# One 512-column matmul for the high and low activations in the dense units of a hybrid encoder block's RWKV pairs

## The reference

```
xn   = rms_norm(h, norm_pre_mix)
cols = xn @ w_in                     # q | k | v | r k v + LoRA-down (RWKV-7) | two merge gates
o_attn = banded_gqa_attention(q, k, v, sink)
o_rwkv = rwkv7_bidirectional(rw_cols, ...)   # token shift, forward scan + backward scan, 32 heads of 64
merged = sigmoid(gate_attn) * o_attn + sigmoid(gate_rwkv) * o_rwkv
h = h + rms_norm(merged @ w_out, norm_post_mix)
h = h + rms_norm(square(relu(rms_norm(h) @ w_ffn_up)) @ w_ffn_down, norm_post_ffn)
```

## Time and profile before

| | |
|---|---|
| runs before | 2079.17, 2077.74, 2077.78 us; median 2077.78 us |
| profiled execution, its own time | 2075.58 us |
| its span, first to last instruction | 2073.8 us |
| busy in the span | PE 1983.6, PE weight loads 1832.3, DVE 1319.7, ACT 927.0, POOL 362.2 us |
| mean granted TensorE clock | 0.988 |

### The profile page before, as it was taken

How to read it: one execution, slowest core, us unless ns; L and a number is a source line. 1 busy time by engine, 2 the same in 40 slices (tenths; PEclk the granted TensorE clock), 3 DMA queues, 4 the chain that set the end, 5 groups by cost and what they waited for, 6 DMA issues and landing times.

```text
span 2073.8 us, 39272 instructions
## 1 busy us (share of the span) xinstructions
PE 1983.6 (96%) x14475; PEld 1832.3 (88%) x14475; DVE 1319.7 (64%) x2218; ACT 927.0 (45%) x1669; POOL 362.2 (17%) x432
## 2 busy tenths in 40 slices
PE   6999999899999999999999999699999999999995
PEld 6999999899999999999999888689898988989894
DVE  3666556677777777777777864655555555555554
ACT  4555433444444444444444544444443434444342
POOL 0000000343333343333334531000000000000000
PEclk9999999999999999999999999899999999999998
DMA  7555666433332233333321327356566565666652
GB/s 207 136 144 139 179 164 166 109 88 87 87 85 80 77 82 87 87 87 87 83 77 41 128 83 245 99 185 184 188 186 188 184 182 183 182 187 183 189 188 81
DMA packets 415087, 281.28 MB, mean 136 GB/s; under 512 B 14042, under 2 KB 372668, under 8 KB 414012
## 3 DMA queue, kind: packets, MB, share of 16 engines
q1 hardware_dynamic: 414620, 277.43, 46.3%
q10 hardware_dynamic: 416, 3.15, 0.4%
HBM read 278.46 MB, written 2.10 MB: 135 GB/s over the span
## 4 chain that ended last, share of the span: by engine, by line
PE 54%; issue 38%; DVE 3%; ACT 2%; POOL 1%; DMA 0%; SPq 0%; ACTq 0%; POOLq 0%; DVEq 0%
PE bank L1483 10%; PE bank L1484 9%; PE bank L1485 9%; PE bank L1724 2%; PE bank L1768 2%; PE bank L1786 2%; PE bank L1791 2%; PE bank L1629 1%; PE bank L1853 1%; PE bank L1631 1%; PE bank L1832 1%; PE bank L1630 1%; DVE G L1121 1%; PE bank L1894 1%; PE bank L1557 1%
## 5 line engine op out<-in xcount | busy, mean ns | idle before, releaser
L1483 PE MATMUL bank<-xT,whi 128*128 128x256 f32 x2784 | 823.2, 296 | 10.1 <-DVE wlo L838 6.3
L1484 PE MATMUL bank<-xT,whi 128*128 128x256 f32 x2784 | 789.2, 283 | 0.0
L1485 PE MATMUL bank<-xT,wlo 128*128 128x256 f32 x2784 | 788.6, 283 | 0.0
L1483 PEld LDWEIGHTS bank<-xT,whi 128*128 128x128 f32 x2784 | 535.0, 192 | 13.0 <-issue 6.9
L1484 PEld LDWEIGHTS bank<-xT,whi 128*128 128x128 f32 x2784 | 535.5, 192 | 1.9
L1485 PEld LDWEIGHTS bank<-xT,wlo 128*128 128x128 f32 x2784 | 534.2, 192 | 0.0
L838 DVE TENSOR_TENSOR wlo<-raw,whi 128x1024 fp32r<-128x1024 f32 (+1 forms) x164 | 246.8, 1520 | 60.2 <-ACT whi L436 55.2
L1343 DVE TENSOR_TENSOR wlo<-raw,whi 128x1024 fp32r<-128x1024 f32 x126 | 154.4, 1226 | 201.0 <-ACT whi L806 201.0
L806 ACT ACTIVATE whi<-raw 128x1024 fp32r<-128x1024 f32 x126 | 132.9, 1054 | 218.0 <-PE bank L1503 218.0
L1502 PE MATMUL bank<-wlo,ft 128*128 128x512 f32 x512 | 202.2, 395 | 0.0
L1503 PE MATMUL bank<-whi,ft 128*128 128x512 f32 x512 | 202.2, 395 | 0.0
(11 more groups left out here) (220 smaller groups left out, 3052.2 us busy)
## 6 DMA issues: line engine op xcount, KB each, us to landing
raw<-in_w_in SPq DMA_DIRECT2D x106, 1024.0 KB, 5.9
raw<-in_w_ffn_up SPq DMA_DIRECT2D x64, 1024.0 KB, 6.5
raw<-in_w_ffn_down SPq DMA_DIRECT2D x64, 1024.0 KB, 5.0
raw<-in_w_out SPq DMA_DIRECT2D x16, 1024.0 KB, 5.3
raw<-in_w_in SPq DMA_DIRECT2D x4, 768.0 KB, 4.6
xtok<-in_x SPq DMA_DIRECT2D x2, 1024.0 KB, 5.9
upg<-in_g_up SPq DMA_DIRECT2D x16, 128.0 KB, 3.3
hres<-in_x ACTq DMA_DIRECT2D x1, 2048.0 KB, 12.1
```

Source lines behind the costliest of these rows:

```text
L1483: M(bank[:, 0:T], h, xT[:, k, 0, :], start=k == 0, stop=False)
L1484: M(bank[:, 0:T], h, xT[:, k, 1, :], start=False, stop=False)
L1485: x = M(bank[:, 0:T], l, xT[:, k, 0, :], start=False, stop=k == KT - 1)
```

## The change

In the units of the pairs (64 units, 1024 tiles) the two matmuls that have `whi` as their weights become one of 512 moving columns, `xT[:, k, :, :]`, which writes the whole bank: high x high in columns 0 to 255, high x low in 256 to 511. The third, of 256 columns, adds low x high to the first half. A tile is then two matmuls and two weight loads where it was three and three. To join the halves ACT copies columns 0 to 255 into `raw4` as before, but signals a new semaphore `d_cp`, and a new DVE instruction adds columns 256 to 511 in place and signals `d_evac`. The units of attention, gates, LoRA, the output projection and the FFN stay as they are.

```diff
@@ ACT dense @@
-                A.activation(raw4[:, slot, 1:T + 1], PB[u % 2][:, 0:T], ACT.Copy).then_inc(d_evac.sem, 1)
+                A.activation(raw4[:, slot, 1:T + 1], PB[u % 2][:, 0:T], ACT.Copy).then_inc(s["d_cp"].sem, 1)
@@ DVE @@
+            def dense(j, i):
+                if isinstance(i, int) and i >= PAIRS:
+                    return
+                u = U_RW + j
+                dve.wait_ge(s["d_cp"].sem, s["d_cp"].at(i, j + 1))
+                row = raw4[:, (1, 0, 2, 3)[j], 1:T + 1]
+                V.tensor_tensor(row, row, PB[u % 2][:, T:2 * T], ALU.add).then_inc(d_evac.sem, 1)
@@ DVE pair @@
+                        if l == 3 and d == 0:
+                            dense(2, d1)
...
+                dense(3, d1)
                 if nx:
                     nx.differences()
                     nx.shift()
...
                             nx.inverse(0)
+                        dense(0, d2)
+                        if nx:
                             nx.modified()
...
                 cut_pair(0, d2, 1)
+                dense(1, d2)
                 cut_pair(1, d2, 0)
@@ DVE ahead of the loop @@
             for j in range(4):
+                dense(j, 0)
                 cut_pair(j, 0)
...
                     g0.bonus()
+                    dense(0, 1)
                     cut_pair(0, 1)
+            dense(1, 1)
             cut_pair(1, 1)
@@ PE dense @@
-                unit_b(U_RW + j, 4 * n + U_RW + j, k0, k1, s["x_free"] if last else None)
+                for k in range(k0, k1):
+                    M(bank[:, :], hi[:, P * k:P * k + P], xT[:, k, :, :], start=k == 0, stop=False)
+                    x = M(bank[:, 0:T], lo[:, P * k:P * k + P], xT[:, k, 0, :], start=False, stop=k == KT - 1)
```

More of the change, by code:

```diff
@@ L256, in block_kernel @@
             ex=4, esink=4, den=4, rden=4, prn=4, p_tp=4, p_T=4, pv=4, o_ev=4,
-            ga_m=4, lo_nb=1, lo_df=1, lo_sh=1, lo_act=1, lo_fin=1, drv=1, zr=1,
+            ga_m=4, lo_nb=1, lo_df=1, lo_sh=1, lo_act=1, lo_fin=1, drv=1, zr=1, d_cp=4,
             up_ld=1, sh_nb=1, sh_df=1, shifted=1, gate_t=1, sqd=1, ss=1, ssm=1, rs=1, rrep=1, rbc=1, nkk=1, gg=2,
@@ L1473, in _, with unit_b @@
             M = nc.tensor.matmul
-            def unit_b(u_static, u, k0=0, k1=KT, half_read=None):
+            def unit_b(u_static, u, k0=0, k1=KT):
                 if k0 == 0:
@@ L1485, in unit_b @@
                     x = M(bank[:, 0:T], l, xT[:, k, 0, :], start=False, stop=k == KT - 1)
-                    if half_read is not None and k == KT // 2 - 1:
-                        x.then_inc(half_read.sem, 1)
                 if k1 == KT:
@@ L1641, in dense @@
                     return
+                u_static, u = U_RW + j, 4 * n + U_RW + j
                 if k0 == 0:
-                    pe.wait_ge(d_evac.sem, d_evac.n(4 * n + U_RW + j - 1))
-                last = isinstance(n, int) and n == PAIRS - 1 and j == 3
-                unit_b(U_RW + j, 4 * n + U_RW + j, k0, k1, s["x_free"] if last else None)
+                    pe.wait_ge(d_evac.sem, d_evac.n(u - 1))
+                    pe.wait_ge(w_lo.sem, w_lo.n(u + 1))
+                bank = PB[u_static % 2]
+                hi, lo = whi[:, u_static % 2, :], wlo[:, u_static % 2, :]
+                for k in range(k0, k1):
+                    M(bank[:, :], hi[:, P * k:P * k + P], xT[:, k, :, :], start=k == 0, stop=False)
+                    x = M(bank[:, 0:T], lo[:, P * k:P * k + P], xT[:, k, 0, :], start=False, stop=k == KT - 1)
+                    if isinstance(n, int) and n == PAIRS - 1 and j == 3 and k == KT // 2 - 1:
+                        x.then_inc(s["x_free"].sem, 1)
+                if k1 == KT:
+                    x.then_inc(w_used.sem, 1)
             inc = lambda x, name: x.then_inc(s[name].sem, 1)
```

## The result

| | before | changed |
|---|---|---|
| median of the runs | 2077.82 us (4 runs, 2077.74 to 2079.17) | 2066.67 us (4 runs, 2064.28 to 2067.07) |
| profiled execution, its own time | 2075.58 | 2066.83 |
| its span | 2073.8 | 2065.0 |

The ratio is 0.9944, with a 95% interval of 0.9929 to 0.9958: 11.15 us faster. The forecast was 5.7 us faster, 2072.1, with 2069.3 as the fast end of its range.

A forecast was written before the change was run, and what follows sets the result against it. PE, busy 96% of the span, was taken as the bound through its matmul issue. Gains of 4.7 (loop), 0.4 (pair 0) and 0.6 (POOL's DT first) summed to 5.7 us, giving 2072.1; range 2069.3 to 2078.0.

The forecast's parts named there:

- The tile: Pairs' units on PE: one matmul of 512 and one of 256 instead of three of 256, 6 ns less per tile.
- The count of tiles that pay, 54 of 64: Loop pair: 10 of 64 tiles lie ahead of places where PE waits for others and gain nothing; 54 gain.
- The adds are free: DVE's 64 new adds, 0.42 us each, were expected to fit into idle time in all four units of a loop pair.
- Unit 3's wait: DVE, ahead of `differences`: waits for ACT's copy, so `differences` and `shift` end 1.5 us later; claimed free.
- unit 1's slack: DVE, ahead of the third half cut: of 0.80 us idle before the Gram matrices, 0.08 is left; claimed free.
- The slower rival: Unit 3's wait on DVE delays the token shift or ACT: up to 1.5 us a pair, 2093 us; chance 0.05.
- the one of unit 0: Rival: the add ahead of `kk`, slack 0.27, is exposed by 0.34 to 0.42 a pair, 2077 to 2078 us; chance 0.09.
- The loop's sum, 4.7 us: Loop: 14 pairs of 54 tiles plus 22 in another pair, 778 tiles at 6 ns, 4.7 us gained.
- Ahead of the loop, 0.4 us for pair 0's units: Pair 0's four units ahead of the loop: 64 tiles at 6 ns, 0.4 us gained, their adds hidden under ACT's cuts.
- I count 0.6, since PE was busy until then, with up to 2: Ahead of the loop: unit 1's add lets POOL's DT precede DVE's cut, removing PE's 0.63 us wait; 0.6 gained.
- The median put at 2.2 above the profiled execution: Whole kernel: the median of runs lies 2.2 us above the profiled execution, so its forecast 2069.9 becomes 2072.1.
- the port: Ahead of the loop: POOL's DT and DVE's cut hold each other up, whoever is first; 0.6 us gained, up to 2.

The follow-up runs named there:

- e2: Changed kernel without the DVE adds, ACT signalling `d_evac` itself and high x low left out of the result: 2073.69 us, ratio 0.9975 to before.
- e1: Changed kernel with the adds kept but each tile done in three matmuls of 256 columns again: 2070.08 us, ratio 0.9964 to before.
- e3: Changed kernel with DVE's cut put ahead of the add of unit 1, ahead of the loop: 2073.24 us, ratio 0.998 to before.
- e6: Kernel before with one useless DVE instruction of 512 columns ahead of the cut that stands ahead of the loop: 2070.14 us, ratio 0.9965.
- e8: e3 with pair 0 taken out of PE's loop and 16 useless matmuls where PE waits for POOL's DT: 2068.78 us, ratio 0.9953 to before.
- e12: Changed kernel with one useless DVE instruction of 512 columns far ahead of the loop: 2067.97 us, ratio 0.9946 to before.
- e10: e5 with each group's 512-column matmuls issued before its 256-column ones, in pairs and up projection: 2053.41 us, ratio 0.9879 to before.
- e5: Changed kernel with the FFN's up projection (64 units) given the wide matmul and DVE add too: 2059.95 us, ratio 0.9912 to before.
- e7: Kernel before with one useless DVE instruction of 512 columns in each loop pair, ahead of the third half cut: 2076.60 us, ratio 0.9992.
- e9a: Kernel before with one useless DVE instruction of 512 columns far ahead of the loop: 2077.62 us, ratio 0.9997.
- e11: Kernel before with two useless DVE instructions of 256 columns far ahead of the loop: 2076.59 us, ratio 0.9983.
- e9b: Kernel before with one useless DVE instruction of 512 columns behind the last pair: 2076.42 us, ratio 1.0.

## Why the prediction was off, step by step

- **The tile**: right. 6.1 ns for 6.
- **The count of tiles that pay, 54 of 64**: right as far as it can be seen. e2, which has before's stall and no adds, has a pair of 53.04, 0.32 less than before: 52 tiles x 6.1 ns.
- **The adds are free**: nearly. Changed (52.93 to 52.95) against e2 less the stall (53.04 - 0.13 = 52.91): 0.02 to 0.04 a pair, some 0.4 us in all. Unit 3's wait (0.94), the `rhs` add's idle time (1.59) and kh ahead of PE are as written, and unit 1's slack was 0.26, not 0.08, the 0.69 that the wait has without the stall less the add. The slower rival and the one of unit 0 didn't come.
- **The loop's sum, 4.7 us**: e1 against the changed kernel is 3.4 us by the medians and 14 x 0.286 = 4.0 by the pairs. Right in kind and about in size.
- **Ahead of the loop, 0.4 us for pair 0's units**: open. The stretch from the first tile of x to the LoRA tiles varies from 348.9 to 352.5 us over the profiles with the draws of the clock, which hides it.
- **Missing: the stall in each pair**, 14 x 0.13 = 1.8 us. No term of the forecast had it. Its mark, DVE's G waiting 0.2 for "issue", stood in the view of waits of before, and its place is the idle time of 0.80 in the earlier trace rows; I had not looked at either as something that a change of the program could shorten.
- **The step that failed is "I count 0.6, since PE was busy until then, with up to 2".** The mechanism, DT first and the cut second, was right, and the size was wrong by a factor of ten: by the swap of e3 it is 6.6 us, by e6 7.75 - 1.8 = 5.95. Two things were wrong in it. The wait of 0.63 was read from a profile in which PE's tiles ahead of DT ran at half the clock (the first row below), so that PE came to DT late; the seven other profiles with the cut first and nothing put into PE's wait have waits of 2.11 to 2.14. And I priced a wait at its own length. Behind the 0.63 of that profile the clock is full; behind the seven others it is 0.50 for 6.8 to 13.7 us. e8 splits the first levels of e3: 1.8 us for DT's lateness, 5.9 for the half clock that follows PE's idle time.

```profile
398.30:401.70 3.40, 3.40 (x18) 0.50 1.00 280
```

- **The median put at 2.2 above the profiled execution**: right for before only. The profile of before has first levels of 23.87 us, where the seven others with that wait have 26.2 to 29.7, and before's own runs, in the sets of 12 to 21 that stand beside the experiments, spread over 5.8 to 6.8 us. With DT first the first levels are 22 to 23 us in every profile, and the changed kernel's profile lies at its median. So a median run of before probably has longer first levels than the profiled one, and the 2.4 us that the spans do not show would lie there. That isn't shown: the second profile of before has 26.21 and is still 1.2 us faster than the first, since its part ahead of the LoRA tiles is 3.3 us shorter, and no run at the median was profiled.
- **The range** was too narrow at its fast end for the reason of the failed step: its fast end had "2 us ahead" of the loop as the most that the port could bring.

Sum by the runs: 6.6 (order and clock, e3) + 1.8 (stall) + 3.4 (wide matmul net of the adds, e1) = 11.8, or with 5.95 by e6 11.15, against 11.15 measured. That the second comes out to the digit is luck: the terms come from medians whose ratios are each uncertain by about 0.1%, 2 us.

**Open.** Why DVE starts late at that place with some positions of its program and not with others. Fetching of instructions would be an explanation; no row shows it, and e12 found no second position that stalls. How long the half clock lasts behind the same wait of 2.1 us (6.8 to 13.7 us) differs from execution to execution, and I can't say by what.

## What to carry to other kernels

Ask of every wait of PE that goes or comes not only how long it is but what clock the profile shows for the microseconds behind it: here a wait of 2.1 us made the first levels 4.2 to 7.7 us longer than the changed kernel's 22.02, and filling it with useless matmuls won back 5.9 of e3's 7.7. Where a GpSimd instruction on the path is ready together with a long DVE instruction with two SBUF inputs, let GpSimd go first, if need be by putting a short instruction ahead of the long one on DVE. If an edit brings more than its own sum, run it without its purpose, as e1 did, before believing in the purpose.

## What the runs showed of the hardware

- One DVE instruction of 0.43 us without use, ahead of a 2048-column cut, made the kernel 7.75 us faster, 1.8 of it by the stall that went too (e6).
- Behind a wait of PE of 2.11 to 2.14 us the granted clock was 0.50 for 6.8 to 13.7 us in each of seven profiles; with 16 matmuls put into the same wait it stayed at 1.00 (e8).
- In the FFN a matmul of 512 columns takes 228.2 ns from start to start in runs of 16 (e10) and 236.3 ns with a 256 behind it (e5); one of 256 takes 119.9 and 116.9 ns. A tile of both is 5 ns cheaper in runs of 16 than alternating (348.1 against 353.2).
- One or two instructions more at any of the three places tried ahead of it in DVE's program removed a stall of 0.13 us that each of the pairs had (e6, e7, e9a, e11), and one behind it did not (e9b).
